# A two-layer streaming encoder on one core: key/value stage unrolled, residual steps spread thinner, attention's transfers on SyncE

## What is computed

```python
x = x + rmsnorm(h, g_mix_post[l])
f = square(relu(rmsnorm(x, g_ffn_pre[l]) @ w_up[l])) @ w_down[l]
x = x + rmsnorm(f, g_ffn_post[l])
kv = rmsnorm(x, g_kv) @ w_kv          # after layer 0: 8 key heads, 8 value heads, 128 wide
q = rmsnorm(x, g_mix_pre[1]) @ w_q    # layer 1; keys and values also go out as rows
```

## Time and profile before

| what | us |
|---|---|
| median of three runs | 2814.36 (2806.95 to 2817.36) |
| the profiled execution | 2806.98 |
| its span, first to last instruction | 2805.2 |
| TensorE busy, matmuls | 2663.2 (95%) |
| VectorE busy | 1272.6 (45%) |
| ScalarE busy | 753.3 (27%) |
| POOL busy | 241.9 (9%) |
| mean granted clock of TensorE | 0.978 of full |

### The profile page before, as it was taken

How to read it: one execution, slowest core, us unless ns; L and a number is a source line. 1 busy time by engine, 2 the same in 40 slices (tenths; PEclk the granted TensorE clock), 3 DMA queues, 4 the chain that set the end, 5 groups by cost and what they waited for, 6 DMA issues and landing times.

```text
span 2805.2 us, 43408 instructions
## 1 busy us (share of the span) xinstructions
PE 2663.2 (95%) x17021; PEld 2559.9 (91%) x17021; DVE 1272.6 (45%) x2323; ACT 753.3 (27%) x1451; POOL 241.9 (9%) x251
## 2 busy tenths in 40 slices
PE   7998997999999999998999899988999999999997
PEld 6998887999999999998899777767999999999997
DVE  5323564653333333338322666664553333333336
ACT  4111334421111111114211555554421111111113
POOL 0000000011001100110000000000011001100110
PEclk9999998999999999999999999999999999999999
DMA  3324542111111111110332222120111111111111
GB/s 111 96 94 130 139 127 78 46 31 46 45 45 45 45 45 50 47 48 28 100 106 76 85 62 66 57 85 24 46 38 46 45 45 45 45 45 45 45 46 69
DMA packets 253169, 176.60 MB, mean 63 GB/s; under 512 B 14408, under 2 KB 242208, under 8 KB 253072
## 3 DMA queue, kind: packets, MB, share of 16 engines
q1 hardware_dynamic: 199640, 121.88, 14.9%
q10 hardware_dynamic: 53432, 53.38, 5.7%
HBM read 141.05 MB, written 34.12 MB: 62 GB/s over the span
## 4 chain that ended last, share of the span: by engine, by line
PE 72%; issue 15%; DVE 7%; ACT 4%; POOL 1%; DMA 1%; SPq 0%; ACTq 0%; POOLq 0%; DVEq 0%
PE PS L428 22%; PE PS L429 21%; PE PS L430 21%; PE PS L803 3%; ACT P L1364 2%; PE PS L836 1%; PE PS L822 1%; DVE X L1473 1%; DVE AS L1960 1%; DVE Y L1471 1%; DVE XL L1462 1%; PE PS L480 1%; ACT WH L948 0%; DVE SQ L1493 0%; PE PS L812 0%
## 5 line engine op out<-in xcount | busy, mean ns | idle before, releaser
L428 PE MATMUL PS<-XH,WH 128*128 128x352 f32 x2928 | 960.1, 328 | 13.3 <-DVE WL L1439 7.3
L430 PE MATMUL PS<-XH,WL 128*128 128x352 f32 x2928 | 944.3, 323 | 0.0
L429 PE MATMUL PS<-XL,WH 128*128 128x352 f32 x2928 | 943.8, 322 | 0.0
L428 PEld LDWEIGHTS PS<-XH,WH 128*128 128x128 f32 x2928 | 554.1, 189 | 18.3 <-issue 9.0
L429 PEld LDWEIGHTS PS<-XL,WH 128*128 128x128 f32 x2928 | 555.0, 190 | 0.0
L430 PEld LDWEIGHTS PS<-XH,WL 128*128 128x128 f32 x2928 | 553.0, 189 | 0.0
L428 PE MATMUL PS<-HH,WH 128*128 128x352 f32 x1440 | 470.1, 326 | 6.6 <-DVE WL L1439 5.1
L430 PE MATMUL PS<-HH,WL 128*128 128x352 f32 x1440 | 468.2, 325 | 0.0
L429 PE MATMUL PS<-HL,WH 128*128 128x352 f32 x1440 | 466.2, 324 | 0.0
L948 ACT ACTIVATE WH<-WR 128x1024 fp32r<-128x1024 f32 x182 | 192.2, 1056 | 824.3 <-PE PS L430 591.5
L1439 DVE TENSOR_TENSOR WL<-WR,WH 128x1024 fp32r<-128x1024 f32 x182 | 222.7, 1225 | 254.6 <-ACT WH L948 254.6
(11 more groups left out here) (231 smaller groups left out, 2329.5 us busy)
## 6 DMA issues: line engine op xcount, KB each, us to landing
WR<-in_w_up SPq DMA_DIRECT2D x64, 512.0 KB, 4.0
WR<-in_w_down SPq DMA_DIRECT2D x64, 512.0 KB, 3.4
proj_s<-STG ACTq DMA_DIRECT2D x24, 528.0 KB, 2.7
WR<-in_w_in_a SPq DMA_DIRECT2D x24, 512.0 KB, 3.7
WR<-in_w_kv SPq DMA_DIRECT2D x16, 512.0 KB, 3.8
out<-OT ACTq DMA_DIRECT2D x16, 512.0 KB, 3.3
CH<-proj_s SPq DMA_DIRECT2D x6, 1024.0 KB, 8.0
OG<-proj_s ACTq DMA_DIRECT2D x8, 528.0 KB, 4.2
```

The costliest lines, as they stand in the source:

```text
L428: pe.matmul(out, lh, rh, start=start, stop=False)
L429: pe.matmul(out, lh, rl, start=False, stop=False)
L430: return pe.matmul(out, ll, rh, start=False, stop=stop)
```

## The change

Three parts. **Last pass of the first MLP**: from item 11 on, a residual step stands at every second item only; seventeen instead of eleven follow the last item. The statistics' order becomes y0, y1, y2, x0, x1, x2, and x0 moves into the boundary. **Key/value stage**: the boundary holds four units (weights of units 2 and 3 go to spare room in `HH`, `HL`), unit 4 runs with the x2 statistic behind its groups, and units 5 to 15 are written out without a loop. Units are taken into a ring of four buffers (`STG`, `STG2`), and their rows are turned in single pieces (`row_op`: 4, 4 and 1 transposes) behind groups of later units, in the order that `row_ops` gives: two pieces a group until the backlog is worked off (units 5 to 8), then one. VectorE splits the low half ahead of a unit's third take. Unit 15 runs block outer, so that the query's halves can be written behind it; its own rows are turned in the first query unit. **Attention**: SP issues the transfers of heads 1 to 7, the outputs and their reading back, between the weight loads; head 0's are issued by ScalarE during the key/value units.

```diff
+            with ExitStack() as under:
+                OT = sb("OT", [P, 2, NCH, P], F32, under)
...
+            with ExitStack() as under:
+                STG2 = sb("STG2", [P, 2, T], F32, under)
...
+        def row_ops(n, g):
+
+            h = 3 * (n - 5) + g
+            end = lambda h: min(2 * (h + 1), 3 * (4 + h // 3) + h % 3 + 1)
+            return range(end(h - 1) if h else 0, end(h))
...
             def steps(self, i):
 
                 i -= self.first
+                if self.b == BOUNDS["b1"]:
+                    return [(i - 11) // 2] if i >= 11 and i % 2 else []
                 js = [i - 11] if self.mlp else [2 * i - 10, 2 * i - 9]
                 return [j for j in js if j >= 0]
...
+            def head_in(h, s):
+
+                sp.wait_ge(sem("a_exp"), 2 * (9 * h - 6))
+                sp.dma_start(KK[:, s, 0:SEQ], kT_s[h][:, 0:SEQ]).then_inc(sem(f"k_in{s}"), 16)
+                sp.dma_start(KK[:, s, SCOL:NKEY], kT_s[h][:, SEQ:T]).then_inc(sem(f"k_in{s}"), 16)
+                sp.wait_ge(sem("a_ckT"), h)
+                sp.dma_start(CK[:, :, :], ck[h]).then_inc(sem("ck_in"), 16)
+                if h >= 2:
+                    sp.wait_ge(sem("a_out"), 9 * (h - 1))
+                sp.dma_start(VV[:, s, 0:NT, :], vp[h]).then_inc(sem(f"v_in{s}"), 16)
+                sp.dma_start(VV[:, s, NT:NT + 4, :], cv[h]).then_inc(sem(f"v_in{s}"), 16)
+                sp.dma_start(VV[0:DEC, s, NT + 4, :], vs[h]).then_inc(sem(f"v_in{s}"), 16)
+
+            def head_out(h):
+                sp.wait_ge(sem("a_otc"), 3 * h + 3)
+                sp.dma_start(o_s[h], OTS).then_inc(sem("o_st"), 16)
+
+            for w in range(U_Q, U_Q + 4):
+                head_weights(w)
+            for h in range(H - 1):
+                head_in(h + 1, (h + 1) % 2)
+                head_weights(U_Q + 4 + h)
+                if h >= 1:
+                    head_out(h - 1)
+            for k in range(KB - 2):
+                sp.wait_ge(sem("o_st"), 16 * (k + 1))
+                if k >= 2:
+                    sp.wait_ge(sem("x_lo"), KB * SPLITS["wo"] + k - 1)
+                sp.dma_start(STG[:, k % 2, :], o_s[k]).then_inc(sem(f"o_in{k % 2}"), 16)
+            for w in range(U_Q + H + 3, U_WO + KB):
...
-                pe.wait_ge(bank_free, g0 + RING)
+                pe.wait_ge(bank_free, g0 + 3 * n)
...
-                            if (g, s, k) == (1, 0, 5):
+                            if name == "b1":
+                                if (g, s, k) == (0, 2, 1):
+                                    x_sums(name, 0)
+                                if (g, s, k) == (0, 2, 5):
+                                    spread(name, "x0")
+                            if (g, s, k) == ((1, 1, 5) if name == "b1" else (1, 0, 5)):
                                 x_sums(name, 1)
-                            if (g, s, k) == (1, 1, 2):
+                            if (g, s, k) == ((1, 2, 2) if name == "b1" else (1, 1, 2)):
                                 spread(name, "x1")
...
                 if name == "b1":
-                    last_stat(0)
-                    last_stat(1)
+                    unit(0, u0 + 5, g0 + 12, last_stat)
...
-            rows_of(0, 0, True)
-            with pe.Fori(1, N_KV // 2) as i:
-                for s in range(2):
-                    unit(s, 2 * i + (U_KV + s + 1), 6 * i + (G_KV + 3 * s))
-                    rows_of(1 - s, 6 * i + 3 * (s - 1))
-            rows_of(1, 3 * (N_KV - 1))
-
...
+            def row_op(q):
+
+                v, r = q // 3, q % 3
+                pe.wait_ge(bank_free, RING + G_KV + (9 + v if v < 4 else 3 * v + 3))
+                pe.wait_ge(sem("kv_rows"), max(q - 1, 0))
+                if r == 2:
+                    mm = pe.transpose(PS[0:DEC, 6 + q % 2, 0:P], kv_stage(v)[:, SEQ:T], ident[:, :])
+                else:
...
+                    for t in range(4):
+                        c = (4 * r + t) * P
+                        mm = pe.transpose(PS[:, 6 + q % 2, t * P:t * P + P], kv_stage(v)[:, c:c + P], ident[:, :])
+                mm.then_inc(sem("kv_turned"), 1)
+
+            def rows_behind(n):
+                def behind(g):
+                    for q in row_ops(n, g):
+                        row_op(q)
+                return behind
+
+            for n in range(5, N_KV - 1):
+                unit(n % 2, U_KV + n + 1, G_KV + 3 * n, rows_behind(n))
+
+            n = N_KV - 1
+            pe.wait_ge(w_lo, U_KV + n + 1)
+            pe.wait_ge(bank_free, G_KV + 3 * n + 3)
+            for k in range(KB):
+                ws = slice(k * P, k * P + P)
+                for g in range(NG):
+                    mm = three(PS[:, 3 + g, 0:G], WH[:, 1, ws], WL[:, 1, ws], XH[:, k, grp(g)], XL[:, k, grp(g)],
+                               k == 0, k == KB - 1)
+                    if k == KB - 1:
+                        mm.then_inc(mm_done, 1)
+                if k < KB - 1:
+                    mm.then_inc(sem("kv_last"), 1)
+                if k in (2, 5):
+                    rows_behind(n)(k // 3)
+            rows_behind(n)(2)
+
+            def last_rows(k):
+                if 4 <= k < 7:
+                    row_op(3 * N_KV - 7 + k)
+
+            first_pair(U_Q, G_Q, "n2", 1, last_rows)
...
-                    if j == 16:
-                        take_rms(name, "y2")
-                    if j == 15 and not it.mlp:
-                        split_spare(2, u0 // 2 + 1, 0, False)
+                    if j == (8 if it.mlp else 15):
+                        split_spare(0 if it.mlp else 2, u0 // 2 + 1, 0, False)
+                    if j == 10 and it.mlp:
+                        split_spare(1, u0 // 2 + 1, 0, False)
+                    for n, what in ((10, "y2"), (13, "x0"), (20, "x1")) if it.mlp else ((16, "y2"), (21, "x1")):
+                        if j == n:
+                            take_rms(name, what)
                     x_step(name, j, pre)
-                    if j == 20:
-                        take_rms(name, "x1")
...
-            split_hi(0, U_KV // 2 + 1, G_KV + 5)
-            split_hi(1, U_KV // 2 + 1, G_KV + 6)
-            take_rms("b1", "x2")
...
+            def keys_out(n):
+                act.wait_ge(bank_free, RING + G_KV + (9 + n if n < 4 else 3 * n + 3))
...
+            def queries_in(k):
+                act.wait_ge(sem("kv_last"), k + 1) if k < KB - 1 else act.wait_ge(mm_done, G_KV + 3 * N_KV)
+                act.activation(XH[:, k, :], X[:, k, :], ACT.Copy, scale=gcol("mix_pre1", k)).then_inc(sem("x_hi"), 1)
...
+            split_hi(0, U_KV // 2 + 2, G_KV + 9)
+            split_hi(1, U_KV // 2 + 2, G_KV + 10)
+            take_rms("b1", "x2")
+            for n in range(4):
+                keys_out(n)
+            for n in range(4, N_KV - 1):
+                if n >= 5:
+                    for g in range(NG):
+                        for q in row_ops(n, g):
+                            row_op(q)
+                split_hi(n % 2, (U_KV + n) // 2 + 1, G_KV + 3 * n + 3)
+                if 5 <= n <= H:
+                    keys_out(n - 1)
+                if n == 9:
+                    act.wait_ge(sem("kt_st0"), 16)
+                    load_k(0, 0)
+                    load_ck(0)
+                if n == 13:
+                    act.wait_ge(sem("kv_st0"), 32 * 5)
+                    load_v(0, 0)
+            for k in range(KB):
+                queries_in(k)
+                if k in (2, 5, 7):
+                    for q in row_ops(N_KV - 1, k // 3):
+                        row_op(q)
+            split_hi(1, (U_KV + N_KV) // 2, G_KV + 3 * N_KV)
+            for q in range(3 * N_KV - 3, 3 * N_KV):
+                row_op(q)
+            for s in range(4):
+                act.wait_ge(sem(f"kt_st{s}"), 16 * 2)
+            for s in range(2):
+                act.wait_ge(sem(f"kv_st{s}"), 32 * 8)
+            for a in range(2):
+                act.activation(lam[:, 2 + a:3 + a], lam[:, a:a + 1], ACT.Exp).then_inc(sem("lam_exp"), 1)
...
-                if t.i == 2 and more:
-                    load_k(h + 1, 1 - t.hp)
-                    load_ck(h + 1)
-                if t.i == 4 and more:
-                    if not (first and t.hp == 0):
-                        act.wait_ge(sem("a_out"), t.n - 4)
-                    load_v(h + 1, 1 - t.hp)
...
-                    if t.i < H - 2:
-                        k = t.i
-                        act.wait_ge(sem("o_st"), 16 * (k + 1))
-                        if k >= 2:
-                            act.wait_ge(sem("x_lo"), KB * SPLITS["wo"] + k - 1)
-                        act.dma_start(STG[:, k % 2, :], o_s[k]).then_inc(sem(f"o_in{k % 2}"), 16)
...
-            load_k(0, 0)
-            load_ck(0)
-            load_v(0, 0)
...
-                    if out and t.i == OUT_ROUND[2] and not (last and t.hp == 1):
-                        act.wait_ge(sem("a_otc"), 3 * t.h)
-                        act.dma_start(o_s[t.h - 1], OTS).then_inc(sem("o_st"), 16)
...
+            def first_take(n):
+
```

(89 more changed lines are left out.)

77 lines of the change are left out of this document (29 added, 48 removed).

## The result

The changed kernel takes 2790.4 us (median of 5 runs, 2784.1 to 2795.3) against 2810.7 for the kernel before on the same chip (5 runs): ratio 0.9925, 95% interval [0.9903, 0.9948], 20.3 us less. The forecast was 10.4 less, 2804 after 2814.4, with a range that ended at 2791. The sign was right, the size half of what came. The profiled execution takes 2784.1 us, its span 2782.3, 22.9 less than the span before.

The account below looks back on a forecast made before the run. TensorE, busy 95% of the span, was taken as the bound, so gains come only from its idle or lower-clock time. -14.5 + 3.5 + 0.25 = -10.75: 2796.2 us profiled, 2804 for the median, range 2791 to 2814 (80%).

Parts of the forecast that it names:

- the price of the rows in units 5 to 14: Units 5 to 14: rows in three pieces, each with a switch of about 0.2, cost 20.1 us in all.
- Last pass: First MLP's last pass from item 11: group 1's sum comes in time, TensorE ends at 1303.8 instead of 1312.3, 8.5 less.
- Boundary: From the pass's end to unit 5: VectorE ends 5.2 behind TensorE, 7.25 us of waits; unit 5 starts at 1375.0.
- the waits at y2 and x0: Boundary: TensorE loses 0.3 us at the statistic y2 and 0.95 at x0.
- The new wait in units 9 to 14: TensorE waits for VectorE's third take before a unit's rows: 0.75 us for units 9 to 13, 5.2 over units 8 to 14.
- Attention's start: Unit 15 to first score: late lambda step puts the score 6.85 us behind the query; stretch 33.55 instead of 34.3.
- Attention: Attention's transfers: seven issues a head move from ScalarE's queue to SP's; nothing gained, upper bound 22 us in seven heads.
- Its own length: Attention from the first score on takes 364 us as before; if that moves, the forecast is wrong.
- The new waits don't come: Rival, 20%: ScalarE's stores and exponentials overlap more than the rows show; 5.2 + 6 us more gain, 2793.
- VectorE only carries its lag: Rival, 18%: VectorE's lag moves over the end of the pass, no step leaves it; 6 to 8 us less gain, 2811.
- ScalarE freed: Rival, 5%: ScalarE, freed of transfer issues in attention, gives the bound of 22 us; 2782.
- The clock: Rival, 6%: added waits in units 8 to 14 let the granted clock sink there; at 0.90, 15.7 us more, 2820.

Follow-up runs that it names:

- the kernel with the take first: Changed kernel with VectorE's third take of units 8 to 14 put ahead of the weight split: 2786.9 us, ratio 0.9914.
- the run block by block: Units 0 and 1 of the boundary's first two groups done in alternating blocks, on the kernel of the three edits together (2779.5 us): 2781.5 us, ratio 0.9902.

## Why the prediction was too small

**The step that failed** is the price of the rows in units 5 to 14: "the rows come in three pieces, each with a switch of about 0.2: a unit with one row costs 1.63, one with two (units 5 to 8) 2.6". Measured are 1.02 and 1.97 (a unit with two rows is 13.42, from 1373.2 to 1386.62, less 11.45). That is 0.6 in each of ten units, 6.2 us. With it goes the 11.57 for a unit, which was 11.45 (1.2 in ten). The mechanism, three pieces and a new wait, was right; this term was too large. The prediction does not show how 1.63 comes about; the 1.03 of the eight transposes and three switches of 0.2 make it. But 1.03 is a duration, and from start to start eight transposes take 0.79; and instead of a switch of 0.2 a piece has only a matmul behind it that starts 0.09 late. Two pieces of four and one single, 2 x 0.44 + 0.12 = 1.00, are the 1.02 measured. The old 1.55 was no better guide. It divides by ten what holds nine rows (15.4 / 9 = 1.71), and it has two things in it that the change removes: the wait listed as 0.25 within the rows, where the ninth transpose starts 0.50 behind the end of the eight by the same 0.79 (1488.29 after 1487.79), and the loop's turn, a gap of 0.27 to 0.30 behind every second unit's rows in TensorE's timeline. The prediction took the wait out in words, and the switches put as much in again.

**The other terms.** *Last pass*: 26.7 for 26.3, right, and with no wait at y1's sum. *Boundary*: 70.4 for 71.2, close, with small errors both ways. The first unit lost 5.15 (9.57 from 1302.80 to 1312.37 less the 3.82 and 0.6 reckoned), forecast 4.6; the blocks came when forecast, and the rest is the lower clock, with the last block's three matmuls taking 1.05 instead of 0.5. Unit 4's wait for its bank was 1.11, forecast 1.4; the waits at y2 and x0 (1.25) did not come. The granted clock was 0.95; twelve matmuls between 1309.0 and 1314.2 stood about 0.3 apart instead of 0.16, 1.8 us in all, so the 1.7 for it was about right. *The new wait in units 9 to 14*: came as named, by the take, in every unit; against the kernel with the take first it cost 4.5, forecast 5.2. (The six parts of its 4.85 add to 4.77; with that the seven waits come to 4.6.) *Attention's start*: 31.3 for 34.6. The pause was 6.0 for 6.85, the two rows and the matmuls 1.5 cheaper by the same wrong price, and the 1.0 for the clock falls behind this stretch, into the first head, where the clock was 0.50 for 8 us. *Attention*: nothing gained by the transfers, as forecast, and shown within 3 us by the two runs that move them. Its own length, whose moving the prediction had set as a sign of being wrong, was 2.8 longer in the first profile and 1.0 shorter in the second.

Units 5 to 14 and attention's start make 8.0 + 3.3 of the 11.6 that the sum fell short; the price of the rows with the unit's 11.57 makes 8.9 of it. With this price right the forecast would have been about 2795, inside its own range. No run puts the loop back, or takes the boundary's four units apart; what these parts are worth is read from the windows alone.

**The rivals.** "The new waits don't come" gave 2793 and is nearest in time, but for the wrong reason: they came. "VectorE only carries its lag" falls twice, in the result and in the run with a step at every item, whose expectation had made the same mistake. "ScalarE freed" falls with the two runs of the transfers, 22 us being far outside their intervals. "The clock" falls with the 1.00 of the third window.

## What to carry to other kernels

When a change splits a block of work into pieces, take its waits and loop turns out of the old block's price before reckoning the pieces, and price them by the distance from start to start, not by durations; here four transposes between matmuls cost 0.35 and a slower start of 0.09. Ahead of a sum that the bound engine waits for, count all the work on the engine that makes it, and move out what is needed later. Before work goes to an idle engine, look whether that engine's instruction holds up the one that is to be relieved.

## What was not expected of the hardware

GpSimd and VectorE hold each other up in both directions. VectorE's 0.52 and 0.58 became 2.18 and 2.72 beside a split on GpSimd. The other way round, GpSimd's power of three columns takes 0.85 in the changed kernel beside a take from PSUM (at 1334.92), and 2.20 when it starts 0.15 behind a weight split of VectorE:

```profile
1311.77 1.21 DVE L1519 TENSOR_TENSOR HL<-WR,HH 128x1024 fp32r<-128x1024 f32 x1
1311.92 2.20 POOL L2089 TENSOR_TENSOR TV<-TV,half 128x3 f32<-128x3 f32 x1 [19.95 <-DVE TV L1526]
...
1320.06 0.51 DVE L1545 TENSOR_TENSOR Y<-Y,RB 128x352 f32<-128x352 f32 x1
1320.22 1.06 POOL L2089 TENSOR_TENSOR TV<-TV,half 128x3 f32<-128x3 f32 x1 [6.10 <-DVE TV L1526]
```

The second pair is the power of x0 that took 5.28 in the run block by block. Here it starts 0.16 behind the same add, VectorE works on without a gap up to 1333.6, and it takes 1.06, as in the other profiles with this order of statistics. So VectorE's work without a gap does not explain the 5.28 by itself; what did is open.

From the first score of one head to that of the next, the second to seventh heads of attention take 44.0 us or 45.6, with the same instructions. One to three of the six are the longer, and not the same ones in two profiles of one kernel (385.8 and 389.6 us up to W_o's wait). The granted clock falls with them, 0.96 in a longer head of the changed kernel and 1.00 in the next:

```profile
1577.39:1622.96 45.57, 42.50 (x296) 34.88 (x296) 29.08 (x61) 23.07 (x56) 1.79 (x1) 0.96 0.18 55
1622.96:1666.99 44.03, 40.88 (x298) 33.60 (x297) 29.36 (x62) 23.01 (x56) 1.79 (x1) 1.00 0.20 62
```

What starts such a dip is open. It is enough to hide a change of 3 us in the median, so that here the stretch, not the total, decided.
